# Layer-norm column sums and index weights in four groups of 32 output partitions, and a reordered memory-key projection

## Chip, cores and metric

The kernel runs on one core of a Trainium2 chip. The metric is the time of one launch on the device, in microseconds (us). The core's engines are TensorE (PE: matrix products into PSUM; PEld is its loading of the stationary operand), VectorE (DVE), ScalarE (ACT), GpSimd (POOL) and SyncE (SP, which issues most transfers). They run side by side and wait for one another through semaphores.

## The reference

All data is float32, with 512 tokens of width 1024. Two mixing layers come first, then a block with grouped-query attention, a gated recurrence, an expert lookup and a last gate. What the change touches lies in the two mixing layers:

```python
def conformer_conv(u, conv_w, conv_b, g, b):          # first layer, width 1536
    a, gl = jnp.split(u, 2, axis=-1)
    h = a * jax.nn.sigmoid(gl)
    h = <causal depthwise convolution with 31 taps>(h) + conv_b
    return jax.nn.silu(layer_norm(h, g, b))

# first layer (j = 0), second layer (j = 1)
    y_mem = mem_cross_attention(qm, mem_n, w_mkv)     # k, v = split(mem_n @ w_mkv)
    y = jnp.concatenate([y_mix, y_mem], axis=-1) * jax.nn.silu(gate)
    x = layer_norm(ALPHA * x + y @ w_out, pg, pb)

# second layer: an indexer picks 128 keys for each query
    wi = (x @ b_w_in)[..., 8 columns]                 # one weight per index head
    iscore = einsum('bqh,bqhs->bqs', wi, relu(einsum('bqhd,bsd->bqhs', qi, ki)))
    _, sel = lax.top_k(iscore, 128)
```

`layer_norm` takes mean and variance over the feature axis. `mem_n` is the normalised memory of 256 rows, the same for both layers.

## The kernel before

Activations lie feature-major: a tile is 128 features (partitions) by 512 tokens. The convolution's output is 12 such tiles in `Y`, which the kernel calls `yt(c)`. A sum over features is then a sum over partitions and over the 12 tiles, and TensorE makes it with a 128x128 stationary operand of ones: 12 products of 128x512, added up in one PSUM bank, leave the column sums on all 128 partitions. The mean is made so in `MEAN_BANK` (L790), then DVE subtracts it from each tile (L1993), ACT squares each tile into one of four `SIG` buffers (L1370), and TensorE sums the squares into `VAR_BANK` (L802). ACT takes the root (L1376), DVE the reciprocal (L1997) and scales the tiles (L1999), ACT applies gain, bias and SiLU (L1383), and POOL (5 tiles) and DVE (7 tiles, L2003) multiply by the gate.

The gate itself is 16 tiles of 8 products each. `gate_fill` (L674) is a generator that yields after each product, so that these 128 "fills" can be laid by hand between other work on TensorE: 96 of them in the memory attention of the first layer (`att_steps`), 12 between the sums of squares, 20 behind them. ACT applies SiLU to each finished gate tile (`gate_silu`, L1292), and a gate tile's bank is reused only when the tile two before is read out.

The order on each engine is the order of the code. On TensorE it is: attention and fills, 12 mean sums, 12 times one fill and one sum of squares, 20 fills, a wait for `gate_done` 16, `mix_gated` 12 and `at_y` 4, `out_projection` (L737; four quarters of 32 products), `mem_kv` (memory keys L622 and values L651 of the second layer), the transposes of the normed X (L660, in `x_transposes`), the second layer's projections `bfm` and `bspec` (L825), the index weights `WI` (L831), and the index scores (L846).

`WI` is token-major: 8 columns for each of 4 blocks of 128 tokens. It is made with XT, 128 tokens by 128 features at a time, as the stationary operand: 32 products with only 8 columns each.

Behind `out_projection` stands `layer_end` on DVE: residual, layer norm, gain and bias for each of four token blocks, the last of which starts when the last product is read out.

Weights come in 2 MB slots from one stream in DRAM, in the order in which TensorE uses them, into two buffers of `W`. SP loads slot s when slot s - 2 is released (`used`). `SLOTS` and `POS` are the tables that number slots and PSUM bank uses; the numbers in `POS` modulo 4 name banks 0 to 3.

A float32 product appears as two records (two passes) of TensorE in the trace: `x24` at L790 is 12 products.

Of the kernel before, what the change touches and what calls it, by code (L numbers as in the profile page):

```python
# [14 lines left out]
P = 128  # L15
# [54 lines left out]
_number(SLOTS, [("u", 6), ("mkv_a", 2), ("qm_a", 1), ("gate_a", 4), ("out_a", 4), ("mkv_b", 2),  # L70
                ("bfm", 4), ("bspec", 1), ("qm_b", 1), ("gate_b", 4), ("out_b", 4),
                ("aq", 1), ("akv", 1), ("hq", 1), ("hff", 1), ("hfb", 1), ("hg", 1), ("hi", 1),
                ("gate_c", 4), ("up", 2), ("wq", 8), ("ple", 2)])
# [123 lines left out]
def program(nc, x, xT, mem, wstream, fmvec, rows, norm_rows, consts, levels, subkeys, pT, proj, peer_u, peer_v,  # L197
            experts, out):
    with ExitStack() as ctx:
        def sb(name, shape, dt=F32):  # L200
            return ctx.enter_context(nc.sbuf_tensor(name, shape, dt))
# [52 lines left out]
        ONES = sb("ONES", [P, P])  # L254
        WI = sb("WI", [P, NB, IDX_HEADS])
        ST = sb("ST", [P, 64])
        MX2 = sb("MX2", [P, 8])
# [22 lines left out]
        FILL_BANK, OT_BANK, S_BANK = (ps[0], ps[1]), (ps[2], ps[3]), (ps[4], ps[5])  # L280
        MEAN_BANK, VAR_BANK = ps[7], ps[6]

        MB = MK[:, 0, 0:3 * T].rearrange("p (b t) -> p b t", b=3)
        TMP = MK[:, 0, 3 * T:4 * T]


# [118 lines left out]
        squared = sem("squared")  # L405
        squares_used = sem("squares_used")
        scaled = sem("scaled")
# [196 lines left out]
        def _(pe):  # L604
# [35 lines left out]

            def mem_kv(name):
                w = slot(SLOTS[name], 0)
                mt = memT.rearrange("p (k n) -> p k n", k=KD)
                project_fm(w, POS[name], 0, 0, [mt[:, k, :] for k in range(KD)])
                used()
                w = slot(SLOTS[name], 1).rearrange("p (k n) -> p k n", k=KD)
                for b in range(2):
                    pos = POS[name] + 4 + b
# [127 lines left out]
            pe.wait_ge(bank_free, POS["mkv_a"] + 4)  # L776
            mem_kv("mkv_a")
            stage_fm("qm_a", None, 1)
# [4 lines left out]

            ring_drained(POS["out_a"])
            pe.wait_ge(ones_ready, 1)

            def column_sum(c):
                pe.wait_ge(conv_tap, CONV_LOOPED * TAPS if c < CONV_LOOPED else
                           (c // 2) * 2 * TAPS + 2 * TAPS - 1 + c % 2)
                mm = pe.matmul(MEAN_BANK[:, :], ONES[:, :], yt(c), start=(c == 0), stop=(c == CONV_T - 1))  # L790
                if c == CONV_T - 1:
                    mm.then_inc(ln_full, 1)

            fill = gate_fill("a")
            att_steps("a", fill)
            pe.wait_ge(at_pTc, len(ATT_A))
            for c in range(CONV_T):
                column_sum(c)
            for c in range(CONV_T):
                next(fill)  # L800
                pe.wait_ge(squared, c + 1)
                mm = pe.matmul(VAR_BANK[:, :], ONES[:, :], SIG[:, c % 4, :],  # L802
                               start=(c == 0), stop=(c == CONV_T - 1))
                if c < CONV_T - 1:
                    mm.then_inc(squares_used, 1)
            mm.then_inc(ln_full, 1)
# [13 lines left out]
            pos = POS["bspec"]  # L820
            w3 = w.rearrange("p (k n) -> p k n", k=KD)
            for m in range(3):
                bank(pos + m)
                for k in range(KD):
                    mm = pe.matmul(ps[(pos + m) % 4][:, :], w3[:, k, m * P:(m + 1) * P], XT[:, k, :],  # L825
                                   start=(k == 0), stop=(k == KD - 1))
                mm.then_inc(bank_full, 1)
            bank(pos + 3)
            for b in range(NB):
# [5 lines left out]
            used()  # L835

# [426 lines left out]
        def _(act):  # L1263
# [14 lines left out]

            def mem_kv(name, layer):
                for m in range(4):  # L1280
                    drain(POS[name] + m, copy_to(MK[:, layer, m * 256:(m + 1) * 256], 256))
                for b in range(2):
                    drain(POS[name] + 4 + b, copy_to(MK[:, layer, 1024 + b * T:1024 + (b + 1) * T]))

# [73 lines left out]
            mem_kv("mkv_a", 0)  # L1358
            for j in range(4):
# [3 lines left out]

            act.wait_ge(ln_full, 1)
            act.activation(MU[:, 0, :], MEAN_BANK[:, :], ACT.Copy, scale=1.0 / CONV_W).then_inc(ln_copied, 1)
# [7 lines left out]
            act.wait_ge(ln_full, 2)  # L1373
            act.activation(MU[:, 1, :], VAR_BANK[:, :], ACT.Copy, scale=1.0 / CONV_W).then_inc(ln_copied, 1)
            act.wait_ge(var_ready, 2)
# [3 lines left out]
            for c in range(CONV_T):  # L1379
                if c in (4, 8):  # L1380
                    gate_silu(13 + c // 4)
                act.wait_ge(scaled, c + 1)
                act.activation(yt(c), yt(c), ACT.Silu, bias=fm("ln_b", c), scale=fm("ln_g", c)  # L1383
                               ).then_inc(silued, 1)
            out_projection("out_a", 2)
            mem_kv("mkv_b", 1)
            x_transposes("xT_a")

            with act.Fori(0, 2) as i:
                for j in range(8):  # L1390
                    drain(POS["bfm"] + j, lambda b: act.activation(ht(i * 8 + j), b[:, :], ACT.Copy), i, 8)
            for m in range(2):
                drain(POS["bspec"] + m, copy_to(ht(16 + m)))
# [459 lines left out]
        def _(dve):  # L1853
# [35 lines left out]
            ch.link(dve.memset(hp[:, :, 0:TAPS - 1], 0.0))  # L1889
            dve.wait_ge(loaded_const, 48)  # L1890
            with dve.Fori(0, CONV_LOOPED // 2) as i:
                for k in range(TAPS):
                    for j in range(2):
                        c = i * 2 + j
                        if k == 0:
                            hold(dve, "dve", glu_done, c + 1)
                            ins = dve.tensor_scalar(yt(c), hrow(c, k, T), V[:, ds(c * TAPS + FM["conv_w"], 1)],
                                                    V[:, ds(c + FM["conv_b"], 1)], ALU.mult, ALU.add)
                        else:

                            dve.wait_ge(conv_tap, i * (2 * TAPS) + (2 * k + j - 1))
                            ins = dve.scalar_tensor_tensor(yt(c), hrow(c, k, T),  # L1902
                                                           V[:, ds(c * TAPS + (FM["conv_w"] + k), 1)],
                                                           yt(c), ALU.mult, ALU.add)
                        ins.then_inc(conv_tap, 1)
# [766 lines left out]
def lay_out(i):  # L2672
# [5 lines left out]
    w += slots_of(i["a_w_mkv"][0]) + slots_of(aw[:, 3072:3584])  # L2678
    w += slots_of(aw[:, 5120:5632]) + slots_of(aw[:, 3584:5120]) + out_slots(i["a_w_out"][0])
    w += slots_of(i["b_w_mkv"][0])  # L2680
    spec = np.concatenate([bw[:, 2048:2304], bw[:, 2304:2368], bw[:, 2304:2368], bw[:, 2368:2376],
# [41 lines left out]
```

## Time and profile before

| | |
|---|---|
| median of 3 runs | 2964.97 us (2963.43 to 2972.8) |
| the profiled execution | 2962.04 us |
| its span, first to last instruction | 2959.9 us |
| mean granted TensorE clock | 0.976 |
| PE busy | 2761.3 us (93%) |
| DVE busy | 1787.7 us (60%) |
| ACT busy | 765.2 us (26%) |
| POOL busy | 761.6 us (26%) |

Busy shares are averages over stages with very different limits. The stages that the change touches lie between 236 and 704 us of the span, and what an edit is worth there is read from the order of events in that stretch. The profiled execution took 2962.04 us, 2.1 us more than its span and 2.9 us less than the median.

### The profile page before, as it was taken

To read this page: it belongs to the slowest core of one execution; us is meant where nothing else is said; L and a number is where in the kernel's file an instruction comes from. 1 tells how busy PE (TensorE), PEld (TensorE's weight loads), DVE (VectorE), ACT (ScalarE), POOL (GpSimd) and SP (SyncE) were. 2 spreads that over 40 slices of the span, in tenths; PEclk is the share of its full clock that TensorE was granted. 3 is DMA by queue.
4 is the path that set the end of the run, shared out by engine and by line. 5 is a ranking of instruction groups with operands and counts; after the bars stand their busy time and mean duration, and the time that the engine had idled before them with its cause. 6 is when DMAs were issued, how large, how long until landed. Compare 5 with 4: busy or idle time off the path is not lost.

```text
span 2959.9 us, 28589 instructions
## 1 busy us (share of the span) xinstructions
PE 2761.3 (93%) x9498; PEld 1607.2 (54%) x9498; DVE 1787.7 (60%) x3591; ACT 765.2 (26%) x2033; POOL 761.6 (26%) x601
## 2 busy tenths in 40 slices
PE   9999999999999989998889988999999899989986
PEld 4454434445565444445554677878888744434432
DVE  3997633005763133247762566899877777757876
ACT  1113320102232011344441232121344411101222
POOL 0530010000000000003220165344422265535664
PEclk9999999999999999999999999999999999999998
DMA  5131122221011212110112499899866699999996
GB/s 199 57 114 57 57 71 85 86 85 57 29 58 43 85 61 85 60 51 24 40 37 93 142 364 387 332 354 320 319 200 199 199 357 409 409 412 409 392 394 225
DMA packets 125763, 544.44 MB, mean 184 GB/s; under 512 B 13888, under 2 KB 14272, under 8 KB 117568
## 3 DMA queue, kind: packets, MB, share of 16 engines
q0 software_dynamic: 73728, 268.47, 24.2%
q1 hardware_dynamic: 49472, 258.02, 23.4%
q10 hardware_dynamic: 2432, 16.29, 1.4%
q8 instruction: 72, 1.18, 0.2%
q14 instruction: 59, 0.48, 0.1%
HBM read 538.52 MB, written 4.19 MB: 183 GB/s over the span
## 4 chain that ended last, share of the span: by engine, by line
PE 64%; DVE 12%; DMA 11%; ACT 4%; issue 4%; POOL 4%; DVEq 0%; ACTq 0%; SPq 0%; POOLq 0%
PE ps L622 14%; PE ps L1186 8%; PE ps L737 7%; DMA STREAM<-experts 6%; PE ps L674 5%; PE ps L1158 5%; PE ps L977 3%; PE ps L875 2%; DVE X L2491 2%; PE ps L1006 2%; DMA EARLY_V<-peer_v,C 2%; DMA ROW_V<-peer_v,C 2%; PE ps L904 2%; PE ps L1083 2%; ACT ONE L1671 2%
## 5 line engine op out<-in xcount | busy, mean ns | idle before, releaser
L1158 PE MATMUL ps<-XTD,STREAM 128*128 128x256 f32 x2048 | 459.8, 383 | 22.6 <-ACT GD L1664 14.3
L622 PE MATMUL ps<-XT,W 128*128 128x512 f32 (+1 forms) x1216 | 471.8, 548 | 6.9 <-issue 4.5
L1186 PE MATMUL ps<-STREAM,GD 128*128 128x512 f32 x1024 | 454.6, 600 | 23.1 <-DMA STREAM<-experts 19.7
L1158 PEld LDWEIGHTS ps<-XTD,STREAM 128*128 128x128 f32 x2048 | 387.3, 192 | 81.3 <-DMA STREAM<-experts 15.2
L1832 POOL DMA_INDIRECT ROW_U<-peer_u,C x208 | 267.3, 1285 | 393.5 <-DVE DOT L2479 370.3
L622 PEld LDWEIGHTS ps<-XT,W 128*128 128x128 f32 x1216 | 229.6, 190 | 248.0 <-issue 238.4
L1186 PEld LDWEIGHTS ps<-STREAM,GD 128*128 128x128 f32 x1024 | 189.4, 191 | 286.4 <-issue 201.7
L2491 DVE SCALAR_TENSOR_TENSOR X<-ROW_V,WEIGHT,X 128x1024 f32<-128x1024 f32 x208 | 267.3, 1285 | 92.3 <-DMA ROW_V<-peer_v,C 80.5
L2479 DVE CUSTOM_DVE_ANT_0 ROW_U<-ROW_U,XN 128x1024 f32<-128x1024 f32 x208 | 253.7, 1220 | 56.0 <-DMA ROW_U<-peer_u,C 54.7
L1841 POOL DMA_INDIRECT ROW_V<-peer_v,C x208 | 246.6, 1185 | 147.9 <-DVE X L2491 108.9
L737 PE MATMUL ps<-W,Y 128*128 128x512 f32 x512 | 224.3, 599 | 9.7 <-DVE Y L2003 6.1
L674 PE MATMUL ps<-XT,W 128*128 128x512 f32 x448 | 217.1, 596 | 1.6 <-ACT G L1292 1.6
L1804 POOL COPY PR<-H 128x256 f32<-128x256 f32 x4 | 1.4, 396 | 750.1 <-DVE H L2128 750.1
L737 PEld LDWEIGHTS ps<-W,Y 128*128 128x128 f32 x512 | 97.6, 192 | 135.8 <-issue 132.6
L1902 DVE SCALAR_TENSOR_TENSOR Y<-H,V,Y x240 | 165.2, 764 | 0.0
L1619 ACT ACTIVATE ACTED<-DOT 128x1 f32<-128x1 f32 x256 | 50.4, 197 | 358.3 <-DVE DOT L2479 357.4
L1816 POOL TENSOR_TENSOR H<-H 128x256 f32<-128x256 f32 x56 | 48.1, 861 | 313.6 <-ACT H L1522 280.5
L2012 DVE SCALAR_TENSOR_TENSOR X<-X,H 128x512 f32<-128x512 f32 x16 | 11.1, 691 | 180.1 <-ACT H L1277 180.1
L674 PEld LDWEIGHTS ps<-XT,W 128*128 128x128 f32 x448 | 79.5, 192 | 59.2 <-issue 54.8
L1671 ACT ACTIVATE ONE<-ONE,IT 128x128 f32<-128x128 f32 x256 | 81.6, 390 | 104.2 <-DVE ONE L2535 104.2
L2047 DVE TENSOR_SCALAR MK<-SIG,WI 128x256 f32<-128x256 f32 (+2 forms) x3 | 1.3, 420 | 175.6 <-ACT SIG L1401 175.6
L1832 POOL DMA_INDIRECT EARLY_U<-peer_u,C x48 | 53.8, 1120 | 200.2 <-DVE C L2418 134.3
(346 smaller groups left out, 3740.6 us busy)
## 6 DMA issues: line engine op xcount, KB each, us to landing
STREAM<-experts SPq DMA_DIRECT2D x256, 512.0 KB, 6.8
W<-wstream SPq DMA_DIRECT2D x53, 2048.0 KB, 8.5
GD<-wstream ACTq DMA_DIRECT2D x2, 2048.0 KB, 16.0
ROW_U<-peer_u,C POOLq DMA_INDIRECT x208, 10.4
ROW_V<-peer_v,C POOLq DMA_INDIRECT x208, 10.6
XT<-xT SPq DMA_DIRECT2D x8, 256.0 KB, 5.7
W<-wstream SPq DMA_DIRECT2D x8, 256.0 KB, 6.5
X<-x SPq DMA_DIRECT2D x1, 2048.0 KB, 19.1
```

What stands on the lines that cost most here:

```text
L622: mm = pe.matmul(b[:, 0:rhs[k].shape[-1]], w[:, k, m * P:(m + 1) * P], rhs[k], start=(k == 0), stop=(k == KD - 1))
L674: mm = pe.matmul(FILL_BANK[j % 2][:, :], w[:, k, m * P:(m + 1) * P], XT[:, k, :], start=(k == 0), stop=(k == KD - 1))
L737: mm = pe.matmul(ps[pos % 4][:, :], Y[:, (j * KD + k) * T + b * P:(j * KD + k) * T + (b + 1) * P], w[:, k, :], start=(j == 0 and k == 0), ...
L977: mm = pe.matmul(ring(pos)[:, :], XT[:, k, b * P:(b + 1) * P], w[:, k, :], start=(k == 0), stop=(k == KD - 1))
L1158: mm = pe.matmul(UP_BANK[g % 2][:, 0:256], u[:, k, :], XTD[:, k, :], start=(k == 0), stop=(k == KD - 1))
L1186: mm = pe.matmul(acc(b, n)[:, :], GD[:, i * 256 + b * P:i * 256 + (b + 1) * P], STREAM[m % STREAM_RING][:, n * T:(n + 1) * T], start=(i == ...
L1671: ins = act.activation(ONE[q % 2][:, 1, i, :], ONE[q % 2][:, 1, i, :], ACT.Copy, scale=IT[:, 2, 4 * q + i:4 * q + i + 1])
L1832: pool.indirect_dma_start(ROW_U[at][:, :], None, peer_u, bass.IndirectOffsetOnAxis(ap=IDX[:, r:r + 1], axis=0)).then_inc(u_loaded[at], 16)
L1841: pool.indirect_dma_start(ROW_V[at][:, :], None, peer_v, bass.IndirectOffsetOnAxis(ap=IDX[:, r:r + 1], axis=0)).then_inc(v_loaded[at], 16)
L1902: ins = dve.scalar_tensor_tensor(yt(c), hrow(c, k, T), V[:, ds(c * TAPS + (FM["conv_w"] + k), 1)], yt(c), ALU.mult, ALU.add)
L2479: dve.tensor_tensor_reduce(out=ROW_U[at][:, :], in0=ROW_U[at][:, :], in1=XN[:, r // P, :], scale=1.0, scalar=0.0, op0=ALU.mult, op1=ALU.ad ...
L2491: dve.scalar_tensor_tensor(X[:, b, :], ROW_V[at][:, :], WEIGHT[:, r % HELD:r % HELD + 1], X[:, b, :], ALU.mult, ALU.add).then_inc(v_added, 1)
```

## The change

1. The mean sums and the sums of squares are made with 32 columns of ones in place of 128. Each product then fills 32 partitions of the bank. Tile c goes to partitions 32 (c mod 4) and up, so that a round of four products writes four groups of partitions of one bank; three rounds cover the 12 tiles. ACT copies the bank, which holds four partial sums, each 32 times, and one full product with ones adds them up (`parts_summed`). The scale of the copy is divided by 32.
2. The squares go to the 12 first tiles of `H` (the convolution's input, no longer needed) in place of four `SIG` buffers, so that ACT no longer waits for TensorE before it squares.
3. The fills are placed anew: 2 behind the mean rounds, 5, 3 and 3 ahead of the three rounds of squares, 2 behind them, 17 at the end.
4. `mem_kv` is split. The second layer's memory keys stand ahead of `out_projection` and ahead of the wait for `mix_gated`; the values stay behind it. Weight slots, banks and ACT's copies follow.
5. ACT's SiLU of gate tiles 12, 14 and 15 stands earlier among its squares and SiLUs.
6. The index weights are made feature-major first: 8 products with 32 stationary columns of the weights and 512 tokens, in two rounds of four groups, ahead of `bspec`'s other products. ACT copies the bank to `WIT`. Four products with `WIT` as stationary operand and an 8-column selection matrix `SEL` add up the four groups and turn them token-major. DVE makes `SEL` once near the start.

```diff
-              ("out_a", 8), ("mkv_b", 6), ("xT_a", 8),
+              ("mkv_bk", 4), ("out_a", 8), ("mkv_bv", 2), ("xT_a", 8),
...
+            def column_sums(bank_, tiles, n):
+                for c in range(4 * n, 4 * n + 4):
+                    g = 32 * (c % 4)
+                    mm = pe.matmul(bank_[g:g + 32, :], ONES[:, 0:32], tiles(c), start=(n == 0), stop=(n == 2))
+                if n == 2:
+                    mm.then_inc(ln_part, 1)
+            def parts_summed(bank_, src, n):
+                pe.wait_ge(ln_part_copied, n)
+                pe.matmul(bank_[:, :], ONES[:, :], src, start=True, stop=True).then_inc(ln_full, 1)
...
-            for c in range(CONV_T):
-                column_sum(c)
-            for c in range(CONV_T):
-                next(fill)
-                pe.wait_ge(squared, c + 1)
-                mm = pe.matmul(VAR_BANK[:, :], ONES[:, :], SIG[:, c % 4, :],
-                               start=(c == 0), stop=(c == CONV_T - 1))
+            pe.wait_ge(conv_tap, CONV_T * TAPS)
+            for n in range(3):
+                column_sums(MEAN_PARTS, yt, n)
+            fills(2)
+            parts_summed(MEAN_BANK, MU[:, 1, :], 1)
+            for n in range(3):
+                fills((5, 3, 3)[n])
+                pe.wait_ge(squared, 4 * n + 4)
+                column_sums(VAR_PARTS, ht, n)
+            fills(2)
+            parts_summed(VAR_BANK, MU[:, 1, :], 2)
             for _ in fill:
                 pass
             pe.wait_ge(gate_done, 16)
+            pe.wait_ge(at_y, 4)
+            mem_keys(SLOTS["mkv_bk"], POS["mkv_bk"])
             pe.wait_ge(mix_gated, CONV_T)
-            pe.wait_ge(at_y, 4)
             out_projection("out_a")
-            mem_kv("mkv_b")
+            mem_values(SLOTS["mkv_bv"], POS["mkv_bv"])
             x_transposes("xT_a", NB)
...
+            for n in range(2):
+                for g in range(4):
+                    mm = pe.matmul(WI_PARTS[32 * g:32 * g + 32, :], w3[:, 4 * n + g, 3 * P:3 * P + 32],
+                                   XT[:, 4 * n + g, :], start=(n == 0), stop=(n == 1))
+            mm.then_inc(wi_part, 1)
...
             for b in range(NB):
-                for k in range(KD):
-                    mm = pe.matmul(ps[(pos + 3) % 4][:, b * IDX_HEADS:(b + 1) * IDX_HEADS],
-                                   XT[:, k, b * P:(b + 1) * P], w3[:, k, 3 * P:3 * P + IDX_HEADS],
-                                   start=(k == 0), stop=(k == KD - 1))
+                mm = pe.matmul(ps[(pos + 3) % 4][:, b * IDX_HEADS:(b + 1) * IDX_HEADS],
+                               WIT[:, b * P:(b + 1) * P], SEL[:, :], start=True, stop=True)
...
+            parts_copied(MEAN_PARTS, 1)
+            act.activation(MU[:, 0, :], MEAN_BANK[:, :], ACT.Copy, scale=1.0 / (32 * CONV_W)).then_inc(ln_copied, 1)
             for c in range(CONV_T):
                 act.wait_ge(centred, c + 1)
-                if c >= 4:
-                    act.wait_ge(squares_used, c - 3)
-                act.activation(SIG[:, c % 4, :], yt(c), ACT.Square).then_inc(squared, 1)
-                if c == 9:
+                act.activation(ht(c), yt(c), ACT.Square).then_inc(squared, 1)
+                if c == 7:
                     gate_silu(12)
...
             for c in range(CONV_T):
-                if c in (4, 8):
-                    gate_silu(13 + c // 4)
+                if c in (1, 5):
+                    gate_silu(14 + c // 4)
```

On TensorE before, from the last fill of the attention to the first sums of squares (L674 are fills, L790 the mean sums, L802 the sums of squares; a row names line, operation, output and inputs, columns and count):

```order
L719 MATMUL ps<-QC,MK 128x128 x2
L674 MATMUL ps<-XT,W 128x512
L790 MATMUL ps<-Y,ONES 128x512 x12
L674 MATMUL ps<-XT,W 128x512
L802 MATMUL ps<-SIG,ONES 128x512
L674 MATMUL ps<-XT,W 128x512
L802 MATMUL ps<-SIG,ONES 128x512
```

On TensorE of the changed kernel, the same place down to `out_projection` (L685 are fills, L803 the tiled sums, L810 the added products, L629 the memory keys, L748 the output projection):

```order
L730 MATMUL ps<-QC,MK 128x128 x2
L685 MATMUL ps<-XT,W 128x512
L803 MATMUL ps<-Y,ONES 32x512 x12
L685 MATMUL ps<-XT,W 128x512 x2
L810 MATMUL ps<-PR,ONES 128x512
L685 MATMUL ps<-XT,W 128x512 x5
L803 MATMUL ps<-H,ONES 32x512 x4
L685 MATMUL ps<-XT,W 128x512 x3
L803 MATMUL ps<-H,ONES 32x512 x4
...
L685 MATMUL ps<-XT,W 128x512 x17
L629 MATMUL ps<-H,W 128x256 x32
```

The 24 sums before are 24 tiled sums and two whole ones now, with fewer changes between fills and sums, and the 32 products of the keys stand behind the last 17 fills.

On ACT of the changed kernel, from the copies of the mean to the memory keys (L1402 copies partial sums, L1409 squares, L1324 is the SiLU of a gate tile, L1422 the layer norm's SiLU, L1307 the copy of a projection's bank):

```order
L1402 ACTIVATE PR<-ps 128x512
L1406 ACTIVATE PR<-ps 128x512
L1409 ACTIVATE H<-Y 128x512 x8
L1324 ACTIVATE G<-ps 128x512
L1409 ACTIVATE H<-Y 128x512 x4
L1402 ACTIVATE PR<-ps 128x512
...
L1422 ACTIVATE Y<-Y,V 128x512
L1324 ACTIVATE G<-ps 128x512
L1422 ACTIVATE Y<-Y,V 128x512 x4
L1324 ACTIVATE G<-ps 128x512
L1422 ACTIVATE Y<-Y,V 128x512 x7
L1307 ACTIVATE MK<-ps 128x256 x4
```

The SiLU of the last gate tile stands behind 5 of the 12 tiles; before, it stood behind 8.

On TensorE of the changed kernel, the second layer's special projections (L849 the tiled index weights, L855 the other projections, L863 the four products with the selection matrix, L671 transposes):

```order
L849 MATMUL ps<-XT,W 32x512 x8
L855 MATMUL ps<-XT,W 128x512 x24
L863 MATMUL ps<-SEL,MK 128x8 x4
L671 MATMUL ps<-C,H 128x128 x4
```

Before, 32 products of 8 columns (L831) stood between the 24 projections and the transposes; now 8 products of 512 columns stand ahead of the 24, and 4 of 8 columns behind them.

## Rows read from the trace of the kernel before

**Rows 1.** The page of the profile: the span and its instructions.

```profile
span 2959.9 us, 28589 instructions
```

**Rows 2.** Chain that ended last, around the sums: start us, us, what.

```profile
338.91 0.86 PE ps L674 x2
340.03 10.55 PE ps L790 x24
350.61 0.61 ACT PR L1365
...
352.72 1.12 PE ps L802 x2
...
372.76 0.60 ACT PR L1374
```

**Rows 3.** Timeline of TensorE behind the sums; in brackets idle time before, and its releaser.

```profile
372.56 17.33 PE L674 MATMUL ps<-XT,W 128*128 128x512 f32 x40
396.02 30.21 PE L737 MATMUL ps<-W,Y 128*128 128x512 f32 x64 [6.13 <-DVE Y L2003]
```

**Rows 4.** Busy time by stretch, with granted clock, DMA share and GB/s.

```profile
core 0: us, PE busy (x) PEld busy (x) DVE busy (x) ACT busy (x) POOL busy (x), PEclk, DMA share, GB/s
...
396.00:402.00 6.00, 5.98 (x8) 2.57 (x9) 0.00 (x0) 0.00 (x0) 0.00 (x0) 0.58 0.15 60
...
678.00:690.00 12.00, 11.74 (x67) 11.44 (x67) 0.00 (x0) 0.80 (x2) 0.00 (x0) 0.62 0.00 1
```

**Rows 5.** Chain that ended last, from the output projection to the memory values.

```profile
426.45 27.74 PE ps L737 x64
...
511.13 14.05 PE ps L622 x64
...
525.47 13.97 PE ps L651 x32
```

**Rows 6.** Chain that ended last, at the second layer's special projections.

```profile
657.57 20.84 PE ps L825 x48
678.41 11.03 PE ps L831 x64
```

**Rows 7.** Line L941: products with 64 stationary columns, two groups of partitions in turn.

```profile
L941 PE MATMUL ps<-Y,H x64: 379/379/430, 1247.8 to 1328.1; 128*64 128x256 f32 x64
```

**Rows 8.** Chain that ended last, around one such group of products.

```profile
1246.13 1.72 PE ps L904 x4
1247.85 1.88 PE ps L941 x16
1249.73 1.06 PE ps L918 x4
1250.79 1.91 PE ps L904 x4
```

**Rows 9.** Timeline of DVE through the layer norm of the convolution.

```profile
351.31 7.31 DVE L1993 TENSOR_TENSOR Y<-Y,PR 128x512 f32<-128x512 f32 x12 [11.63 <-ACT PR L1365]
...
378.72 12.69 DVE L1999 TENSOR_TENSOR Y<-Y,PR 128x512 f32<-128x512 f32 x12
391.34 4.29 DVE L2003 TENSOR_TENSOR Y<-Y,G 128x512 f32<-128x512 f32 x7
```

**Rows 10.** DMA issues from 330 to 560 us: size, median us to landing.

```profile
W<-wstream SPq DMA_DIRECT2D x8, 2048.0 KB, 8.4
```

**Rows 11.** Timeline at the end of the output projection: ACT's last copy, DVE's last step.

```profile
510.68 0.60 ACT L1277 ACTIVATE H<-ps 128x512 f32<-128x512 f32 x1 [4.15 <-PE ps L737]
...
515.74 1.22 DVE L2032 TENSOR_TENSOR X<-X,SIG 128x1024 f32<-128x1024 f32 x1
```

**Rows 12.** Groups by form: the first taps of the convolution on DVE; busy, mean ns, idle before.

```profile
L1897 DVE TENSOR_SCALAR Y<-H,V x8 | 6.8, 873 | 28.2 <-POOL H L1790 28.0 <-issue 0.2
```

**Rows 13.** Line L831 alone in two short stretches: busy, records, clock.

```profile
678.30:680.30 2.00, 2.00 (x20) 2.00 (x19) 1.00 0.00 0
684.00:686.00 2.00, 2.00 (x11) 2.00 (x10) 0.50 0.00 0
```

More of the change, by code:

```diff
@@ L255, in program @@
         WI = sb("WI", [P, NB, IDX_HEADS])
+        SEL = sb("SEL", [P, IDX_HEADS])
         ST = sb("ST", [P, 64])
@@ L280, in program @@
         FILL_BANK, OT_BANK, S_BANK = (ps[0], ps[1]), (ps[2], ps[3]), (ps[4], ps[5])
-        MEAN_BANK, VAR_BANK = ps[7], ps[6]
+        MEAN_PARTS, VAR_PARTS, MEAN_BANK, VAR_BANK = ps[7], ps[6], ps[4], ps[5]
+        WI_PARTS = ps[5]
         MB = MK[:, 0, 0:3 * T].rearrange("p (b t) -> p b t", b=3)
         TMP = MK[:, 0, 3 * T:4 * T]
+        WIT = TMP
         def tm(region, first, width, b, a=0, n=None):
@@ L405, in program @@
         squared = sem("squared")
-        squares_used = sem("squares_used")
+        ln_part = sem("ln_part")
+        ln_part_copied = sem("ln_part_copied")
+        sel_ready = sem("sel_ready")
+        wi_part = sem("wi_part")
+        wi_copied = sem("wi_copied")
         scaled = sem("scaled")
@@ L639, in stage_fm, with mem_keys, mem_values @@
                     used()
[L641 to L644, printed above, removed]
+            mt = memT.rearrange("p (k n) -> p k n", k=KD)
+            def mem_keys(s, pos0):
+                project_fm(slot(s, 0), pos0, 0, 0, [mt[:, k, :] for k in range(KD)])
                 used()
-                w = slot(SLOTS[name], 1).rearrange("p (k n) -> p k n", k=KD)
+            def mem_values(s, pos0):
+                w = slot(s, 0).rearrange("p (k n) -> p k n", k=KD)
                 for b in range(2):
-                    pos = POS[name] + 4 + b
+                    pos = pos0 + b
                     bank(pos)
@@ L782, in ring_drained, with fills @@
                 pe.wait_ge(bank_free, pos + 4)
-            ring_drained(POS["out_a"])
+            ring_drained(POS["mkv_bk"])
             pe.wait_ge(ones_ready, 1)
[L787 to L792, printed above, removed]
+            def column_sums(bank_, tiles, n):
[7 more added lines that the diff above has]
+                pe.matmul(bank_[:, :], ONES[:, :], src, start=True, stop=True).then_inc(ln_full, 1)
+            def fills(n):
+                for _ in range(n):
+                    next(fill)
             fill = gate_fill("a")
@@ L827, in _ @@
                 mm.then_inc(bank_full, 1)
+            used()
             bank(pos + 3)
+            pe.wait_ge(wi_copied, 1)
+            pe.wait_ge(sel_ready, 1)
             for b in range(NB):
-                for k in range(KD):
-                    mm = pe.matmul(ps[(pos + 3) % 4][:, b * IDX_HEADS:(b + 1) * IDX_HEADS],
-                                   XT[:, k, b * P:(b + 1) * P], w3[:, k, 3 * P:3 * P + IDX_HEADS],
-                                   start=(k == 0), stop=(k == KD - 1))
+                mm = pe.matmul(ps[(pos + 3) % 4][:, b * IDX_HEADS:(b + 1) * IDX_HEADS],
+                               WIT[:, b * P:(b + 1) * P], SEL[:, :], start=True, stop=True)
             mm.then_inc(bank_full, 1)
-            used()
             pe.wait_ge(bank_free, POS["bfm"] + 14 + 4)
@@ L1277, in copy_to, with mem_keys, mem_values @@
                 return lambda b: act.activation(dst, b[:, 0:n], ACT.Copy)
-            def mem_kv(name, layer):
+            def mem_keys(pos, layer):
                 for m in range(4):
-                    drain(POS[name] + m, copy_to(MK[:, layer, m * 256:(m + 1) * 256], 256))
+                    drain(pos + m, copy_to(MK[:, layer, m * 256:(m + 1) * 256], 256))
+            def mem_values(pos, layer):
                 for b in range(2):
-                    drain(POS[name] + 4 + b, copy_to(MK[:, layer, 1024 + b * T:1024 + (b + 1) * T]))
+                    drain(pos + b, copy_to(MK[:, layer, 1024 + b * T:1024 + (b + 1) * T]))
             def block_root(b, n):
@@ L1362, in _, with parts_copied @@
             att_steps("a")
-            act.wait_ge(ln_full, 1)
-            act.activation(MU[:, 0, :], MEAN_BANK[:, :], ACT.Copy, scale=1.0 / CONV_W).then_inc(ln_copied, 1)
+            def parts_copied(parts, n):
+                act.wait_ge(ln_part, n)
+                if n == 2:
+                    act.wait_ge(ln_full, 1)
+                act.activation(MU[:, 1, :], parts[:, :], ACT.Copy).then_inc(ln_part_copied, 1)
+                act.wait_ge(ln_full, n)
+            parts_copied(MEAN_PARTS, 1)
+            act.activation(MU[:, 0, :], MEAN_BANK[:, :], ACT.Copy, scale=1.0 / (32 * CONV_W)).then_inc(ln_copied, 1)
             for c in range(CONV_T):
                 act.wait_ge(centred, c + 1)
-                if c >= 4:
-                    act.wait_ge(squares_used, c - 3)
-                act.activation(SIG[:, c % 4, :], yt(c), ACT.Square).then_inc(squared, 1)
-                if c == 9:
+                act.activation(ht(c), yt(c), ACT.Square).then_inc(squared, 1)
+                if c == 7:
                     gate_silu(12)
-            act.wait_ge(ln_full, 2)
-            act.activation(MU[:, 1, :], VAR_BANK[:, :], ACT.Copy, scale=1.0 / CONV_W).then_inc(ln_copied, 1)
+            parts_copied(VAR_PARTS, 2)
+            act.activation(MU[:, 1, :], VAR_BANK[:, :], ACT.Copy, scale=1.0 / (32 * CONV_W)).then_inc(ln_copied, 1)
             act.wait_ge(var_ready, 2)
@@ L1391, in _ @@
                     drain(POS["bfm"] + j, lambda b: act.activation(ht(i * 8 + j), b[:, :], ACT.Copy), i, 8)
+            act.wait_ge(wi_part, 1)
+            act.activation(WIT, WI_PARTS[:, :], ACT.Copy).then_inc(wi_copied, 1)
             for m in range(2):
@@ L1890, in _ @@
             dve.wait_ge(loaded_const, 48)
+            dve.tensor_reduce(SEL[:, :], ident.rearrange("p (g h) -> p h g", g=4)[:, 0:IDX_HEADS, :], AX.X, ALU.add
+                              ).then_inc(sel_ready, 1)
             with dve.Fori(0, CONV_LOOPED // 2) as i:
@@ L2678, in lay_out @@
     w += slots_of(i["a_w_mkv"][0]) + slots_of(aw[:, 3072:3584])
-    w += slots_of(aw[:, 5120:5632]) + slots_of(aw[:, 3584:5120]) + out_slots(i["a_w_out"][0])
-    w += slots_of(i["b_w_mkv"][0])
+    keys, values = slots_of(i["b_w_mkv"][0])
+    w += slots_of(aw[:, 5120:5632]) + slots_of(aw[:, 3584:5120]) + [keys] + out_slots(i["a_w_out"][0]) + [values]
     spec = np.concatenate([bw[:, 2048:2304], bw[:, 2304:2368], bw[:, 2304:2368], bw[:, 2368:2376],
```

14 lines of the change are left out of this document (7 added, 7 removed).

## The prediction

> **What bounds the kernel now.** The page gives the span, 2959.9 us [rows 1], and the table a TensorE that is busy for 93% of it, so I read the chain of work that ended last, in order of time, from the end of the first layer's attention to the index scores. It runs on TensorE except for a few links. The last fill of the attention ends at 338.91 + 0.86 = 339.77 us; then come the 12 mean sums (24 passes, 10.55 us), ACT's copy, a short trip over DVE and ACT, and the sums of squares between fills [rows 2]. After the copy of the variance TensorE's timeline shows 20 more fills (40 passes, 17.33 us) and a hole of 6.13 us that ends with DVE's last gate product [rows 3]. In the hole the granted clock falls: it is 0.58 on average over the 6 us behind it [rows 4], that is mostly 1.2 GHz and not 2.4, and the first quarter of the output projection takes 30.21 us [rows 3] where the second takes 27.74 [rows 5]. The hole costs 6.1 + 2.5 us. Much later, the index weights take 11.03 us on the same chain [rows 6].
>
> One pass of 512 columns at full clock is 17.33 / 40 = 0.43 us [rows 3], so a float32 product is 0.86 us.
>
> **Do four groups of partitions run side by side?** Everything hangs on this, and the trace has no product with 32 stationary columns. It has one with 64 [rows 7]: two groups of 64 partitions of one bank, 256 columns, 16 passes. One after the other, 16 passes of 256 columns would take 16 x 0.215 = 3.4 us. The chain shows 1.88 us [rows 8], which is 8 x 0.215 = 1.72 and 0.16. Two groups overlap fully. The next two pieces also change the shape of the tiles, and are long by 1.06 - 0.86 = 0.20 (row groups of 64) and 1.91 - 1.72 = 0.19 [rows 8]. So a change of tile shape costs about 0.19 us each way. For four groups the bounds are 0.86 us a round (all four together) and 3.44 us (none together, as four whole products); between them lies 1.72 (two together). I take 0.86, since the nearest row shows no loss at all from sharing a bank, the stationary loads or the streams, and a round of four asks for no more passes per us (8 in 0.86, 9.3 per us) than that row had (16 in 1.88, 8.5 per us).
>
> A rule of the Trainium skill speaks against it. "TensorE: Matmul & The Clock Gate" (Part 3, The mechanism) says that the load of a stationary operand overlaps products in flight only where the row groups differ; here all groups use all 128 rows. By that rule the products would run in series with their loads exposed. The trace disagrees for two column groups: 1.88 us for what in series is at least 3.4 [rows 8]. I keep it as a rival.
>
> **The first layer, step by step.** Before, from 339.77 to the end of the memory values at 525.47 + 13.97 = 539.44 [rows 2, 5], is 199.7 us. The same work in the changed kernel on TensorE:
> - gap ahead of the sums as before, 340.03 - 339.77 = 0.26;
> - 32 fills of 0.86: 27.5;
> - six rounds of tiled sums of 0.86: 5.1 (24 products were 20.6);
> - two added products with ones: 1.7;
> - eight changes of tile shape at 0.19 (into and out of four places): 1.6;
> - a wait for the last gate SiLU, worked out below: 0.9;
> - memory keys, 14.05 [rows 5] and 0.4 of gaps: 14.5;
> - output projection: a warm first quarter of 27.74 and 0.2, then 426.45 to 511.13, 84.7 [rows 5]: 112.6;
> - memory values: 14.0.
>
> The sum is 178.2 us, so 21.5 are gained. Of it 15.5 is the tiling of 24 sums, less 1.7 and 1.6 for what it adds; 6.1 and 2.5 are the hole and the slow clock behind it; the rest is small waits (the first sum of squares waited: 350.58 to 352.72 with one fill in it, 1.3 [rows 2]) against the new 0.9.
>
> Whether the covers hold:
> - ACT's copy of the partial sums (0.6, and 0.3 from the last pass to it, as between 340.03 + 24 x 0.43 = 350.35 and 350.61 [rows 2]) is hidden by two fills, 1.7 us. Without them it would cost 0.9 twice.
> - Mean chain: sums end at 342.8, two fills, one product, ACT's copy starts near 345.9 in place of 350.61 [rows 2]. Centring is 7.31 us for 12 tiles [rows 9], and squares now follow it at the same pace. Four squares are there at 350, eight at 352.5, twelve at 355.6. TensorE reaches the rounds at 350, 353.8 and 357.6. No wait over 0.2.
> - The variance's copy then starts at 361.7, 11.1 earlier than 372.76 [rows 2]. Eps, root and reciprocal take the same 378.72 - 372.76 = 6.0, so scaling starts at 367.7 and ends 12.7 later at 380.4; DVE's seven gate products take 4.3 [rows 9] and `mix_gated` is complete near 384.7.
> - Fills end 17 x 0.86 behind 361.4, at 376.0. ACT has five SiLUs done at about 373 and waits there for the last gate tile, 376.3, takes 0.6 as its copies do, and TensorE goes on at 376.9. That is the 0.9. Queued behind ACT's wait are seven SiLUs, done by 382.5, which leaves 384.7 as it is.
> - Keys run from 376.9 to 391.0. The last gate product is 6 us earlier: the hole is filled by work that had to be done anyway. If the variance chain came more than 6 us later, the rest would return as a hole.
> - Weights: slot 14 (first half of the output projection) is asked for when the gate's last slot is released, 376.0; a load takes 8.4 to land [rows 10], 384.4, and it is wanted at 391. Before, it had been loaded long ago. 6.6 us in hand.
> - Layer end: DVE's last step ends at 516.96, 6.3 behind ACT's last copy at 510.68 [rows 11]. Its cover shrinks from 28 us (keys and values) to 14.0 (values). 7.7 in hand, so the move costs nothing there.
> - DVE's `SEL`, one small reduction near the start, stands ahead of the first taps, for which DVE idles 28.2 us until POOL delivers [rows 12]. It costs nothing; without that cover it would be at most the 0.61 of a centring, a full tile [rows 9].
>
> **The index weights.** Before, 657.57 to 689.44, 31.9 us [rows 6]. Now: two rounds 1.7, two changes of shape 0.4, projections 20.84, and 8 passes of 8 columns. At full clock 20 such passes took 2.0 us [rows 13], so 0.9 with a gap. The copy to `WIT` is hidden by 20.84 us of projections. The sum is 23.9: 8.0 gained. Part of the old 11.03 was the clock, which fell in this stretch (0.62 [rows 4]; 11 passes in 2 us in place of 20 [rows 13]). It may now fall in the index scores behind it, which are short products too, and cost up to 2 us there or give up to 1; I take nothing.
>
> **Sum.** 21.5 + 8.0 = 29.5 us. All later work hangs on TensorE's place in this chain, so it passes to the end. The profiled execution of 2962.0 becomes 2932.5; the median lies 2.9 above it, so 2935.4.
>
> **The rivals.**
> - Four groups overlap only two at a time (12%). For: the trace shows only two. Against: nothing in that row is used up. Eight rounds cost 0.86 more each: +6.9, 2942.
> - No overlap (5%). Then 8 rounds cost 2.58 more: +20.6, 2956. Still ahead, since hole and slow clock are filled.
> - No overlap, and each load of a stationary operand exposed (3%). Half a change of shape, 0.1, for each of 64 passes is 6.4 more: 2962, within 0.3% of before. This is what the rule of "TensorE: Matmul & The Clock Gate" in the Trainium skill, above, would make of the change.
> - Slower (2%): the change of tile shape. Ten are added. At 0.19 they cost 1.9. At 3.1 us each they eat the gain, and at 4.0 the kernel is slower by 0.3%. The Trainium skill's "TensorEngine Tiling (Array Packing)" (Key Properties) says that a change of mode drains the engine; the trace agrees that it costs something. For this rival speaks nothing but that no row has 32 columns; the three changes in the rows cost 0.16 to 0.20 us [rows 8].
> - A cover fails (4%): weights or the gate chain are late by a few us and the hole returns in part; 2938 to 2946.
>
> **Numbers.** My forecast, four together and the covers holding, has 74%: 2935, with 2928 to 2942 as its own range, from the clock (it falls for a few us at many holes of the trace, and a kernel shifted by 30 us meets other ones, two or three falls more or less at 2.5 us) and from the median, which moved by several us between three runs. The range 2927 to 2948 takes in two at a time and part of the failed covers, and leaves out the two serial rivals. A measurement of this kernel can tell about 0.3%, 9 us, from no change: faster needs less than 2956. The first case, two at a time, failed covers and half of no overlap give 0.93 for faster, 0.05 for the same, 0.02 for slower.
>
> **What would show it.** A round of four tiled sums: 8 passes starting within 0.9 us, the first four almost together. The copy of the variance near 362, a first quarter of the output projection of 27.7 us with no hole over 1 us ahead of it and a clock of 1.00. The memory values' end near 518. Index weights of 2.1 us ahead of the projections and under 1.1 behind. Wrong would be: passes of the tiled sums 0.43 us apart one by one, a releaser by SP or ACT of more than 2 us ahead of the keys or the projection, or transposes that wait for DVE.

## The result, and the profile after

The changed kernel takes 2936.32 us (median of 5 runs, 2934.69 to 2939.39) against 2963.43 us (5 runs, 2958.83 to 2972.8). The ratio is 0.9905, 95% interval 0.9892 to 0.9917: about 28 us faster (25 to 32), where 29.5 were forecast. The profiled execution took 2937.61 us, with a span of 2935.5.

The chain that ended last, in the first layer of the changed kernel (start us, us, what; L685 fills, L803 tiled sums, L810 the added products, L1324 the last gate SiLU, L629 memory keys, L748 output projection, L662 memory values):

```profile
342.31 2.78 PE ps L803 x24
345.09 1.91 PE ps L685 x4
347.00 0.86 PE ps L810 x2
347.86 4.29 PE ps L685 x10
352.15 1.00 PE ps L803 x8
353.15 2.77 PE ps L685 x6
...
363.46 14.61 PE ps L685 x34
...
378.08 0.60 ACT G L1324
...
378.74 14.10 PE ps L629 x64
...
393.26 27.73 PE ps L748 x64
...
505.55 13.97 PE ps L662 x32
```

These answer to [rows 2, 3, 5]. The 12 mean sums take 2.78 us where 12 whole ones took 10.55. A round of four takes 1.00 us. The six fills between two rounds (three products) take 2.77 and not 2.58: 0.19 for a change of tile shape. Between the last fill and the keys stands one SiLU and a wait of 0.69. The output projection follows 0.4 us behind the keys, and its first quarter takes 27.73 us.

The tiled sums alone in short stretches of the first round of squares (PE busy with records in flight, PEld the same, clock, DMA):

```profile
352.00:352.12 0.12, 0.04 (x4) 0.04 (x6) 1.00 0.00 0
352.12:352.50 0.38, 0.38 (x4) 0.12 (x8) 1.00 0.00 0
352.50:352.70 0.20, 0.20 (x8) 0.00 (x0) 1.00 0.00 0
```

Four passes start within the first 0.12 us, no other until 352.50, and then the other four. The records don't name the pass. Since the two passes of one product write the same group, I read them as the first passes of four products together, and then the second ones.

DVE in the same part, and its last step of the layer end:

```profile
348.60 7.31 DVE L2037 TENSOR_TENSOR Y<-Y,PR 128x512 f32<-128x512 f32 x12 [6.66 <-ACT PR L1406]
369.45 12.68 DVE L2043 TENSOR_TENSOR Y<-Y,PR 128x512 f32<-128x512 f32 x12
382.06 4.29 DVE L2047 TENSOR_TENSOR Y<-Y,G 128x512 f32<-128x512 f32 x7
...
510.15 1.23 DVE L2076 TENSOR_TENSOR X<-X,SIG 128x1024 f32<-128x1024 f32 x1
```

The steps have the lengths of [rows 9, 11]; only their places moved. The last gate product ends at 386.35, 6.9 us before the output projection wants it. The layer end is done at 511.38, 8.1 us before the values end at 519.52.

The second layer's special projections, from TensorE's timeline (L849 tiled index weights, L863 the selection products, L671 transposes, L876 index scores), which answer to [rows 6]:

```profile
637.54 1.93 PE L849 MATMUL ps<-XT,W 128*32 128x512 f32 x16 [0.38 <-issue]
639.39 20.87 PE L855 MATMUL ps<-XT,W 128*128 128x512 f32 x48
660.52 1.03 PE L863 MATMUL ps<-SEL,MK 128*128 128x8 f32 x8 [0.26 <-issue]
661.41 0.63 PE L671 MATMUL ps<-C,H 128*128 128x128 f32 x4
661.97 12.45 PE L876 MATMUL ps<-QC,H 64*128 64x256 f32 x48
```

The clock in three stretches of the changed kernel, just behind the keys, in the special projections and in the index scores (columns as in [rows 4]):

```profile
393.00:399.00 6.00, 5.74 (x14) 2.64 (x15) 0.00 (x0) 0.23 (x1) 0.00 (x0) 1.00 0.82 300
...
637.00:662.00 25.00, 24.36 (x79) 10.82 (x78) 0.00 (x0) 3.18 (x6) 0.00 (x0) 1.00 0.27 92
662.00:674.00 12.00, 12.00 (x49) 6.75 (x48) 10.07 (x20) 10.04 (x22) 0.00 (x0) 1.00 0.39 158
```

Both falls to the lower level (1.2 GHz) that [rows 4] show are gone: the clock reads 1.00, which is 2.4 GHz.

### The profile page after: what moved, and what is told of

Read it like the earlier page. It is cut to its first block, busy times and chain, and to the rows that moved or that the text cites. A ratio compares the mean times of both kernels' runs of the same rounds, so it can differ in the third digit from the quotient of the medians.

```text
span 2935.5 us, 28512 instructions
## 1 busy us (share of the span) xinstructions
PE 2741.0 (93%) x9462; PEld 1589.7 (54%) x9462; DVE 1786.8 (61%) x3592; ACT 766.3 (26%) x2036; POOL 776.4 (26%) x601
## 4 chain that ended last, share of the span: by engine, by line
PE 66%; DMA 12%; DVE 11%; ACT 4%; issue 4%; POOL 3%; DVEq 0%; ACTq 0%; SPq 0%; POOLq 0%
PE ps L629 14%; PE ps L1216 9%; PE ps L748 7%; DMA STREAM<-experts 6%; PE ps L685 6%; PE ps L1188 6%; PE ps L1007 3%; DMA ROW_V<-peer_v,C 3%; PE ps L905 2%; PE ps L1036 2%; DVE X L2535 2%; PE ps L934 2%; PE ps L1113 2%; ACT ONE L1713 2%; PE ps L1101 2%
## 5 line engine op out<-in xcount | busy, mean ns | idle before, releaser
L629 PE MATMUL ps<-XT,W 128*128 128x512 f32 (+1 forms) x1216 | 471.8, 548 | 6.9 <-issue 4.5
L629 PEld LDWEIGHTS ps<-XT,W 128*128 128x128 f32 x1216 | 229.6, 190 | 248.0 <-issue 238.4
L1883 POOL DMA_INDIRECT ROW_V<-peer_v,C x208 | 235.4, 1132 | 158.1 <-DVE X L2535 122.4
L748 PE MATMUL ps<-W,Y 128*128 128x512 f32 x512 | 221.8, 594 | 3.7 <-ACT H L1307 1.4
L685 PE MATMUL ps<-XT,W 128*128 128x512 f32 x448 | 216.7, 598 | 1.6 <-ACT G L1324 1.6
L748 PEld LDWEIGHTS ps<-W,Y 128*128 128x128 f32 x512 | 96.6, 190 | 127.8 <-issue 123.9
L1832 POOL TENSOR_TENSOR H<-H,SIG 128x512 f32 x12 | 108.0, 9001 | 79.0 <-ACT SIG L1384 75.5
L685 PEld LDWEIGHTS ps<-XT,W 128*128 128x128 f32 x448 | 79.2, 192 | 60.8 <-issue 56.5
L1706 ACT ACTIVATE GD<-ps 128x256 f32<-128x256 f32 (+22 forms) x127 | 43.2, 341 | 229.2 <-PE ps L1188 229.2
```

The lines of the kernel that those rows point to most:

```text
L629: mm = pe.matmul(b[:, 0:rhs[k].shape[-1]], w[:, k, m * P:(m + 1) * P], rhs[k], start=(k == 0), stop=(k == KD - 1))
L685: mm = pe.matmul(FILL_BANK[j % 2][:, :], w[:, k, m * P:(m + 1) * P], XT[:, k, :], start=(k == 0), stop=(k == KD - 1))
L748: mm = pe.matmul(ps[pos % 4][:, :], Y[:, (j * KD + k) * T + b * P:(j * KD + k) * T + (b + 1) * P], w[:, k, :], start=(j == 0 and k == 0), ...
L1832: pool.tensor_tensor(hrow(i * 4 + j, TAPS - 1, T), hrow(i * 4 + j, TAPS - 1, T), SIG[:, j, :], ALU.mult).then_inc(glu_done, 1)
L1883: pool.indirect_dma_start(ROW_V[at][:, :], None, peer_v, bass.IndirectOffsetOnAxis(ap=IDX[:, r:r + 1], axis=0)).then_inc(v_loaded[at], 16)
```

## The experiments

Six kernels take the change apart; behind them stand the two kernels themselves once more. The times were taken beside the kernel before on the same chip. Of each edit the telling lines are shown, and "..." marks what is left out.

**Only the sums tiled** (`sums_only`): keys behind the output projection, index weights as before. The squares in `H`, the places of the fills and of ACT's gate SiLUs stay as in the changed kernel. The edit against the changed kernel:

```diff
-            mem_keys(SLOTS["mkv_bk"], POS["mkv_bk"])
             pe.wait_ge(mix_gated, CONV_T)
             out_projection("out_a")
+            mem_keys(SLOTS["mkv_bk"], POS["mkv_bk"])
...
```

> Only the tiled sums of the layer norm; memory keys behind the output projection and index weights as before. My theory (overlap of four groups takes 15.5 us off TensorE and 11.1 off the variance chain, but the memory keys are needed to fill the hole that this leaves): the variance chain sets the start of the output projection, at about 384.7 us of the span in place of 396.0 (each moved by what the stages ahead of it differ, at most 2.3 us); a hole of 8 to 9 us stands ahead of it, the clock falls behind it and the first quarter takes about 30 us. Gain 11.3 us, a ratio of 0.996. Rival (the tiled sums alone make the gain, and the keys only change places): a gain near 20 us, a ratio of 0.993, no long hole.

Ratio 0.9969 (0.9958 to 0.998), 9.2 us. From TensorE's timeline:

```profile
342.08 2.78 PE L803 MATMUL ps<-Y,ONES 128*32 128x512 f32 x24 [0.26 <-issue]
...
386.56 30.49 PE L748 MATMUL ps<-W,Y 128*128 128x512 f32 x64 [8.74 <-DVE Y L2038]
```

From the first mean sum to the output projection it is 386.56 - 342.08 = 44.5 us, where the kernel before has 396.02 - 340.03 = 56.0: 11.5 less, and 11.3 were expected. The hole grew from 6.13 to 8.74 us and the slow first quarter stayed. TensorE's relief is larger than what the variance chain lets through, and the rival, a gain near 20 us without a long hole, is refuted.

**Only the keys moved** (`keys_only`): sums and index weights as before. The edit against the kernel before:

```diff
+            mem_keys(SLOTS["mkv_bk"], POS["mkv_bk"])
             pe.wait_ge(mix_gated, CONV_T)
             out_projection("out_a")
-            mem_kv("mkv_b")
+            mem_values(SLOTS["mkv_bv"], POS["mkv_bv"])
...
```

> Only the memory keys ahead of the output projection; sums and index weights as before. My theory: fills end at 389.9, the last gate SiLU 0.9 later, keys to 405.2, output projection from there with a warm first quarter; the hole of 6.1 us and 2.5 us of slow clock go, a wait of 0.9 comes: gain 7.6 us, ratio 0.9974. Rival (the slow clock comes anyway, from the keys' short products or elsewhere): gain near 5 us, first quarter at 30 us.

Ratio 0.9969 (0.9957 to 0.9981), 9.2 us. The chain:

```profile
390.38 14.10 PE ps L629 x64
...
404.94 27.73 PE ps L748 x64
```

The keys start at 390.38 and the projection at 404.94 with a warm first quarter, as worked out. The timing's size is a little over the 7.6 expected, within its interval (5.6 to 12.7 us). In the trace the stretch from the end of the attention to the end of the values is 531.20 - 339.58 = 191.6 us against 199.7, 8.1 less. The unchanged index weights also came out shorter in this profile:

```profile
670.01 9.76 PE L844 MATMUL ps<-W,XT 128*128 128x8 f32 x64
```

By their timelines they took 11.18 and 11.32 us in the two profiles of the kernel before and 10.91 in `sums_only`. The granted clock over the stage was 0.71 on average in `keys_only` and 0.61 to 0.64 in those three: how much of the stage runs at the lower level differs between profiles.

**Only the index weights** (`index_only`): sums and keys as before. From the edit against the kernel before:

```diff
+                    mm = pe.matmul(WI_PARTS[32 * g:32 * g + 32, :], w3[:, 4 * n + g, 3 * P:3 * P + 32],
+                                   XT[:, 4 * n + g, :], start=(n == 0), stop=(n == 1))
...
```

> Only the index weights in four groups, the rest as before. My theory: from the first tiled product to the last product with the selection matrix 24 us in place of 31.9, gain 8 to 9 us, ratio 0.997. Rival (the clock then falls in the index scores behind it, or the top-k on VectorE absorbs it): gain below 5 us, and the stage of the index scores longer than its 13.9 us.

Ratio 0.9964 (0.9951 to 0.9977), 10.7 us. From TensorE's timeline:

```profile
397.94 29.77 PE L748 MATMUL ps<-W,Y 128*128 128x512 f32 x64 [6.16 <-DVE Y L2029]
...
658.88 1.93 PE L837 MATMUL ps<-XT,W 128*32 128x512 f32 x16 [0.38 <-issue]
...
683.31 12.45 PE L864 MATMUL ps<-QC,H 64*128 64x256 f32 x48
```

It gives 658.88 for the first tiled product and 683.31 for the first index score, 24.4 us; before it was 690.77 - 657.57 = 33.2 [rows 6 and the transposes behind them]. That is 8.8 us, and the index scores took 12.45 us as in the changed kernel. The rival is refuted.

By the timing the three parts give 9.2 + 9.2 + 10.7 = 29.1 us against 28 together, the same within their intervals.

**All tiled products in one group** (`one_group`): the same 32 columns, but no two can run side by side. All else, the index weights too, is as in the changed kernel. The edit against it:

```diff
-                    g = 32 * (c % 4)
-                    mm = pe.matmul(bank_[g:g + 32, :], ONES[:, 0:32], tiles(c), start=(n == 0), stop=(n == 2))
+                    mm = pe.matmul(bank_[0:32, :], ONES[:, 0:32], tiles(c), start=(c == 0), stop=(c == CONV_T - 1))
...
-                pe.matmul(bank_[:, :], ONES[:, :], src, start=True, stop=True).then_inc(ln_full, 1)
+                pe.matmul(bank_[:, :], ONES[0:32, :], src[0:32, :], start=True, stop=True).then_inc(ln_full, 1)
...
```

> The changed kernel, but all 12 tiled products of a sum write the same 32 partitions, with the same shape of 32 stationary columns, so that no two can run side by side; the added product then uses 32 rows. My theory (the gain of the tiling is overlap alone, not the smaller load or fewer columns): a product takes 0.86 us, the mean sums 10.3 us in place of 2.8 and each round of squares 3.4 in place of 1.0, so 15 us more than the changed kernel, ratio to the kernel before about 0.9955. Rival (products with 32 stationary columns are shorter by themselves): the mean sums take well under 10 us and the kernel is within 5 us of the changed one. If loads are exposed as well, the mean sums take 12 us or more.

Ratio 0.9947 (0.9933 to 0.9961). The chain:

```profile
342.43 10.46 PE ps L802 x24
...
354.80 1.05 PE ps L809 x2
...
360.34 3.55 PE ps L802 x8
...
394.98 14.10 PE ps L629 x64
```

A product takes 10.46 / 12 = 0.87 us with 32 stationary columns, as with 128. The smaller loads of the stationary operand give nothing and are not exposed either; overlap is the whole gain of the tiling. From the first mean sum to the keys it is 394.98 - 342.43 = 52.6 us against 378.74 - 342.31 = 36.4 in the changed kernel: 16.1 more, where 15 were expected. Of it 0.8 us are changes of shape around the added product, which has 32 rows here and takes 1.05 us. The squares in `H` and the new places of the fills are in this kernel too, so they are not what shortens the sums. Of the whole, 0.9947 against 0.9905 and 0.9912 for the changed kernel points the same way.

**Two groups of 64** (`two_groups`). The edit against the changed kernel:

```diff
-                    g = 32 * (c % 4)
-                    mm = pe.matmul(bank_[g:g + 32, :], ONES[:, 0:32], tiles(c), start=(n == 0), stop=(n == 2))
+                    g = 64 * (c % 2)
+                    mm = pe.matmul(bank_[g:g + 64, :], ONES[:, 0:64], tiles(c), start=(c < 2), stop=(c >= CONV_T - 2))
...
-            act.activation(MU[:, 0, :], MEAN_BANK[:, :], ACT.Copy, scale=1.0 / (32 * CONV_W)).then_inc(ln_copied, 1)
+            act.activation(MU[:, 0, :], MEAN_BANK[:, :], ACT.Copy, scale=1.0 / (64 * CONV_W)).then_inc(ln_copied, 1)
...
```

> The changed kernel with the sums in two groups of 64 partitions (64 stationary columns, six rounds of two for each sum) in place of four groups of 32; index weights stay in four groups. My theory (as many products overlap as there are groups, and a round takes one product's 0.86 us): mean sums 5.3 us in place of 2.8, each round of squares (four products) 1.85 in place of 1.0, the kernel 5.1 us slower than the changed one. Rival (two groups already give all there is, and four are bound by something else): the same time as the changed kernel within 1 us in that stretch.

The chain:

```profile
340.11 5.37 PE ps L803 x24
...
352.54 1.87 PE ps L803 x8
...
381.74 14.10 PE ps L629 x64
```

12 products take 10.46, 5.37 and 2.78 us in one, two and four groups; a round of squares 3.55, 1.87 and 1.00. From the first mean sum to the keys it is 381.74 - 340.11 = 41.6 us against 36.4 in the changed kernel: 5.2 more, as expected. The rival, the same time within 1 us, is refuted. The time of the whole, 2940.42 us against 2937.52 for the changed kernel beside it, points the same way, but the intervals overlap (0.9903 to 0.9931, 0.9896 to 0.9928).

**Keys begin before the last gate tile is read out** (`keys_early`). The edit against the changed kernel:

```diff
-            pe.wait_ge(gate_done, 16)
             pe.wait_ge(at_y, 4)
...
+            for half in range(2):
+                if half:
+                    pe.wait_ge(gate_done, 16)
...
```

> The changed kernel, but TensorE waits for the last gate SiLU only ahead of the third and fourth block of memory keys, whose banks the gate used; the first two go to other banks. My theory: the wait of 0.69 us ahead of the keys goes and nothing else moves, output projection 0.7 us earlier, too little for the timing to tell. Rival (ACT, which copies the keys only behind its seven SiLUs, then holds up TensorE): the wait comes back at a later block of the keys or ahead of the output projection.

The chain:

```profile
378.32 0.26 issue
378.58 14.07 PE ps L842 x64
...
393.08 7.13 PE ps L748 x16
```

The wait of 0.69 shrinks to a gap of 0.26, and the stretch from the first mean sum to the output projection from 393.26 - 342.31 = 50.95 to 393.08 - 342.58 = 50.50 us. Nothing comes back later. 0.45 us, of the 0.7 expected, is below what the timing can tell: 2939.7 against 2937.52 us, ratios 0.9913 and 0.9912. This was the only kernel tried that might have been faster than the changed one.

**The changed kernel and the kernel before, once more** (`after_again`, `before_again`).

> The changed kernel once more, timed beside the two above, with a second profile. From the first attention to the index scores it should stand where it stood, within 0.3 us between its own landmarks. Open: the clock fell near 181 us of the span in the first profile of it and not in that of the kernel before. If that belongs to the change it comes again; if to the single execution it may not.

> The kernel before, profiled a second time. In its first profile it lost nothing near 181 us and ran some 5 us faster than five later kernels between 1560 and 2380 us, where nothing was changed. My theory: that was this one execution, so the second profile loses 1 to 2 us near 181 or 3 to 5 us in the later stretch, and the span is nearer to 2962. Rival (the change slows the later stretch, by the phase in which transfers and clock meet it): the second profile equals the first within 1 us at all landmarks.

The changed kernel gave 2937.52 us and 0.9912 (0.9896 to 0.9928), span 2933.7. The kernel before took 2968.66 us in its second profile, span 2966.5 where the first had 2959.9. From the end of the attention to the end of the index scores the second profiles repeat the first: 706.12 - 342.31 = 363.8 us before and 673.90 - 341.59 = 332.3 after. The stretch from 180 to 190 us in the first and the second profile of the kernel before:

```profile
180.00:190.00 10.00, 10.00 (x46) 8.83 (x47) 10.00 (x11) 0.77 (x2) 4.45 (x4) 1.00 0.21 88
```

```profile
180.00:190.00 10.00, 9.17 (x35) 7.78 (x36) 10.00 (x11) 1.44 (x4) 5.90 (x4) 0.83 0.28 119
```

The clock falls there in the second and not in the first, and the first mean sum starts at 342.57 and no longer at 340.03. In all it fell there in 7 of 10 profiles, the kernel before among them. So the 2.3 us by which the changed kernel's first profile is late ahead of the mean sums belong to single executions. The same holds for most of what it seemed to give back later. From the end of the index scores to the end of the span the kernel before took 2256.3 us in its first profile and 2260.4 in its second, the changed kernel 2261.1 and 2259.8, the other six 2257.7 to 2269.2. The first profile of the kernel before was the quickest of the ten there. Whether the change costs a microsecond or two in that later part, these profiles can't tell.

## Why the prediction was right

**Four groups side by side: right.** The bound of 0.86 us a round was the one to take. Measured are 2.78 us for three rounds and 1.00 for one with its change of shape. `one_group` and `two_groups` show that time goes with one over the number of groups.

The step from two groups to four was weaker than it read. The row that decided it had two groups [rows 8]. I wrote that a round of four asks for "no more" passes per us than that row, but 9.3 is more than 8.5. The passes are also twice as long: 8 x 512 columns in 0.86 us are 4760 per us, 16 x 256 in 1.88 are 2180. So the row showed nothing at the rate that four groups need. That the rate was there is a result of the runs, and in the prediction it was in part luck.

The rule of the Trainium skill that I weighed against it ("TensorE: Matmul & The Clock Gate", Part 3, The mechanism), that a load overlaps products in flight only where the row groups differ, does not hold here: loads and products that share all 128 rows overlap in every one of these kernels. The kernel before could have told, for its fills load 128x128 operands for 192 ns each and still follow one another at 0.43 us a pass [rows 3]. From its groups by form:

```profile
L674 PEld LDWEIGHTS ps<-XT,W 128*128 128x128 f32 x448 | 79.5, 192 | 59.2 <-issue 54.8
```

**The first layer: 21.5 us forecast, 22.2 measured.** From the end of the last fill of the attention to the end of the memory values it was 199.7 us and is 519.52 - 342.04 = 177.5, with 178.2 forecast. The eight changes of shape cost 0.17 each on average (2.78 + 3 x 1.00 is 0.6 over six rounds of 0.86, and four stretches of fills are 0.19 over each), 0.19 forecast. The last gate SiLU costs 0.7 where 0.9 was worked out.

**The covers: right, each by its margin.** Last gate product 6.9 us ahead (6 forecast), layer end 8.1 ahead of the values' end (7.7). The projection doesn't wait for weights. The reordering was needed: tiled sums alone pass on 11.5 of their relief and leave 8.74 us of hole.

**The hole and the clock: right.** The slow clock behind the hole, 2.5 us, is gone in every kernel that fills it (27.73 us for the first quarter in `keys_only` and the changed kernel), and stays in both that don't (30.49 us in `sums_only`, 29.77 in `index_only`).

**The index weights: mechanism right, size short.** 8.0 forecast to the last selection product; 661.55 - 637.54 = 24.0 in place of 31.9 gives 7.9. I took nothing for the clock in the index scores behind it, with "up to 2 us there or up to 1 given". It did not fall there. In the kernel before, the transposes and the index scores (TensorE's timeline):

```profile
689.68 1.09 PE L660 MATMUL ps<-C,H 128*128 128x128 f32 x4 [0.26 <-ACT WI L1277]
690.70 12.97 PE L846 MATMUL ps<-QC,H 64*128 64x256 f32 x48
```

The transposes take 0.49 us in the changed kernel's chain in place of 1.09, the scores 12.45 in place of 12.97, and the wait of 0.26 for ACT's copy is gone: some 1.4 us more. Over half of the 7.9 is the clock and not the count of products. At full clock the 64 passes would have taken 64 x 2.0 / 20 = 6.4 us [rows 13], an estimate, where they took 11.03. So about 4.6 us go with the lower level and about 3.3 with the shape.

**The sum.** In the two first profiles, the stretch from the end of the attention to the end of the index scores is 703.61 - 339.77 = 363.8 us before and 674.35 - 342.04 = 332.3 after: 31.5 us, and 31.5 again in the second profiles. The timing says 28 (25 to 32), and the spans of the two pairs of profiles differ by 24.4 and 32.8. These agree at the edge of the interval; where the rest goes, if anywhere, can't be told apart from the spread between executions, of which the two profiles of the kernel before (6.6 us apart) give the size. So that the gain "passes to the end" is shown within this interval and no closer. The measured 2936.32 us lies 0.9 from the 2935.4 forecast, and part of that closeness is luck: the forecast started from a median of 2964.97 us, the kernel before took 2963.43 beside the changed one, and the gain was smaller than forecast.

## What to carry to other kernels

A float32 product with 32 output partitions costs as much as a whole one (0.87 us); put four of them in four groups of 32 partitions of one bank, issue them back to back, and they cost little more than one (2.78 us for three rounds of four). The partial sums then need one copy and one more product, so lay filling work under the copy and keep rounds together, since each switch to or from the tiled shape costs 0.14 to 0.21 us. Before counting on TensorE's relief, follow the chain of the other engines: here it let 11.5 us through and the rest had to be filled with work from behind the wait, which also kept the clock up.

## What the runs showed of the hardware

The two passes of float32 products in four groups start four by four: four starts within 0.12 us, none for 0.4 us, then four more. And the clock: during a stage of 32 short products (8 columns each) it fell from 1.00 (2.4 GHz) to 0.50 (1.2 GHz) in the kernel before [rows 13], and the low level ran on into the transposes behind it, which took 1.09 us in place of 0.49. The same fall is in the three other profiles with these products (`before_again`, `sums_only`, `keys_only`). With 8 products of 512 columns ahead of the projections and 4 short ones behind them, the clock stayed at 1.00 from 637 to 674 us of the changed kernel, through the index scores too, which are short products themselves; so it did in the other profiles with this shape. Why the fall comes with the one and not with the other, these runs don't show.
